# A hybrid encoder block on one core: front, attention and experts' start reordered, operands placed alike

## The reference

```python
mod = silu(c) @ w_ada + b_ada            # 6 vectors of 1024 per group
h = rmsnorm(x) * (1 + scale1) + shift1
proj = h @ w_in                          # 5648 columns
#   qkv_a, z_a, beta, alpha: DeltaNet, 4 heads of 128, both directions, chunks of 64
#   q_b, k_b, v_b: 8 heads of 64, attention in a window of 8 rows x 16 columns of the 8 x 64 grid
merged = sigmoid(gate_a) * (o_a @ w_oa) + sigmoid(gate_b) * (o_b @ w_ob)
x = x + gate1 * (merged @ w_out)
h = rmsnorm(x) * (1 + scale2) + shift2
#   16 experts, each takes its top 64 tokens of each group:
y[idx] += (silu(h[idx] @ w_gate) * (h[idx] @ w_up)) @ w_down * gate
x = x + gate2 * y;  out = rmsnorm(x)
```

## Time and profile before

| | us |
|---|---|
| median of three runs | 2578.36 |
| lowest, highest | 2576.54, 2578.36 |
| the profiled execution's own time | 2572.44 |
| its span | 2570.7 |

### The profile page before, as it was taken

How to read it: one execution, slowest core, us unless ns; L and a number is a source line. 1 busy time by engine, 2 the same in 40 slices (tenths; PEclk the granted TensorE clock), 3 DMA queues, 4 the chain that set the end, 5 groups by cost and what they waited for, 6 DMA issues and landing times. The chain is left out here.

```text
span 2570.7 us, 39210 instructions
## 1 busy us (share of the span) xinstructions
PE 2389.5 (93%) x15048; PEld 1815.6 (71%) x15048; DVE 1508.4 (59%) x1785; ACT 1166.5 (45%) x1296; POOL 447.8 (17%) x396
## 2 busy tenths in 40 slices
PE   4999998899998999989992999999999999999994
PEld 2777887777776777743452888888888888888883
DVE  4566212555553333312115788888888888888884
ACT  4232222222222333321112667776776776767772
POOL 5110202232321000011232011111101111111101
PEclk8999999999998999999995999999999999999997
DMA  7446621001002122164314899999999999999994
GB/s 272 148 141 179 159 79 43 19 20 34 19 31 74 63 86 67 37 234 163 115 66 175 320 369 380 373 372 373 371 370 375 381 376 380 373 376 373 373 363 147
DMA packets 266048, 556.95 MB, mean 217 GB/s; under 512 B 13256, under 2 KB 66605, under 8 KB 262861
## 3 DMA queue, kind: packets, MB, share of 16 engines
q1 hardware_dynamic: 256717, 530.15, 57.4%
q0 software_dynamic: 4608, 16.78, 2.6%
q10 hardware_dynamic: 4608, 8.39, 0.9%
HBM read 511.21 MB, written 44.07 MB: 216 GB/s over the span
## 5 line engine op out<-in xcount | busy, mean ns | idle before, releaser
L2378 PE MATMUL ps<-whigh,xeT 128*128 128x512 f32 x2048 | 668.9, 400 | 9.0 <-DVE xeT L2523 9.0
L2531 DVE TENSOR_TENSOR wlow<-hT,whigh 128x2048 fp32r<-128x2048 f32 x192 | 431.9, 2284 | 84.5 <-ACT whigh L2474 84.5
L2378 PEld LDWEIGHTS ps<-whigh,xeT 128*128 128x128 f32 x2048 | 387.0, 189 | 100.1 <-issue 9.4
L2378 PE MATMUL ps<-wlow,xeT 128*128 128x512 f32 x1024 | 406.6, 397 | 0.0
L2474 ACT ACTIVATE whigh<-hT 128x2048 fp32r<-128x2048 f32 x192 | 358.6, 1911 | 17.8 <-PE ps L2378 17.8
L2378 PE MATMUL ps<-whigh,hidT 128*128 128x512 f32 x1024 | 334.6, 398 | 1.5 <-DVE hidT L2558 1.5
L2531 DVE TENSOR_TENSOR wlow<-oaT,whigh 128x2048 fp32r<-128x2048 f32 x96 | 216.7, 2285 | 50.2 <-ACT whigh L2474 50.2
L2531 DVE TENSOR_TENSOR wlow<-obT,whigh 128x2048 fp32r<-128x2048 f32 x96 | 217.8, 2284 | 29.6 <-ACT whigh L2474 29.6
L2378 PEld LDWEIGHTS ps<-whigh,hidT 128*128 128x128 f32 x1024 | 192.8, 188 | 47.9 <-issue 1.7
L2378 PEld LDWEIGHTS ps<-wlow,xeT 128*128 128x128 f32 x1024 | 193.6, 189 | 43.2
L2378 PE MATMUL ps<-wlow,hidT 128*128 128x512 f32 x512 | 202.8, 396 | 0.0
(11 more groups left out here) (289 smaller groups left out, 3542.4 us busy)
## 6 DMA issues: line engine op xcount, KB each, us to landing
hT<-in_w_down SPq DMA_DIRECT2D x66, 1024.0 KB, 8.8
obT<-in_w_up SPq DMA_DIRECT2D x64, 1024.0 KB, 8.7
hT<-in_w_up SPq DMA_DIRECT2D x64, 1024.0 KB, 6.4
hT<-in_w_gate SPq DMA_DIRECT2D x62, 1024.0 KB, 9.3
oaT<-in_w_down SPq DMA_DIRECT2D x62, 1024.0 KB, 7.2
oaT<-in_w_gate SPq DMA_DIRECT2D x34, 1024.0 KB, 9.3
obT<-in_w_gate SPq DMA_DIRECT2D x32, 1024.0 KB, 5.9
oaT<-in_w_ada SPq DMA_DIRECT2D x20, 1024.0 KB, 7.8
```

Of the source, the lines that this page charges most:

```text
L2378: mm = pe.matmul(out, lhs[x], rhs[y], start=start and i == 0, stop=stop and i == 2)
L2531: dve.tensor_tensor(wlow[slot][:, :], raw[(FIRST + x) % RAW_SLOTS], whigh[slot][:, :].bitcast(F32), ALU.subtract).then_inc(low_done, 1)
```

## The change

- **Front stage.** A sixth buffer for pieces of w_ada, over the third and fourth weight tile's raw buffers. SP loads five pieces, tile 0, three pieces, tile 1, and tile 2 once piece 5 is multiplied. The out_t buffers move ahead of w_high, so that w_high0 and w_low0 lie over pieces 2 and 3. split(0) waits for four pieces only and stands before the copy of modrow on ScalarE and before the mod vectors on VectorE. The mod_dram stores are issued at tile 20.
- **Its end.** The front awaits only the stores of DeltaNet's tiles. DeltaNet's first vnew, which with wT lies over out_t, waits for the others, and SP does before it loads attention's first pair.
- **Attention.** A unit's head is now its fastest index, so units 2s and 2s + 1 are the two heads of one pair on the same tile. A slot s has scores of both, eight gate products, both turns, eight, both values, eight. Sums and reciprocals have four places, the values of a pair one bank.
- **Experts.** ScalarE makes whigh of three pieces and VectorE wlow of two before their parts of xeT, and the other three and four after them.
- **Addresses.** Two unused buffers of 32 bytes, and the places of wg and gst, move ghi and glo to 32 modulo 64, as h_high is, and xeT and hidT to 0 modulo 64, as whigh is.

```diff
-    ADA_SLOT = [0, 1, 2, 3, 4, 0, 1, 4] + [q % 2 for q in range(8, PIECES)]
+    ADA_SLOT = [0, 1, 2, 3, 4, 5, 0, 1] + [q % 2 for q in range(8, PIECES)]
...
+        ada.append(m["obT"][:, 2:4, :].rearrange("p h t -> p (h t)"))
...
-                for q in range(KD):
+                for q in range(5):
                     load_ada(q)
-                for tile in range(3):
-                    load_tile(sp, a, wraw, w_in, tile)
+                load_tile(sp, a, wraw, w_in, 0)
+                for q in range(5, KD):
+                    load_ada(q)
+                load_tile(sp, a, wraw, w_in, 1)
+                sp.wait_ge(ada_ps, 6)
+                load_tile(sp, a, wraw, w_in, 2)
...
+                    if tile == 20:
+                        for part in range(2):
+                            sp.wait_ge(mod_done, part + 1)
+                            for b in range(4):
+                                c = (ADA_FIRST + 4 * part + b) * ADA_BLOCK
+                                sp.dma_start(mod_dram[:, c:c + ADA_BLOCK], brow[32 * b:32 * b + GROUPS, part, :]).then_inc(mod_out, 16)
...
-                    sp.wait_ge(out_kept[i], 16 * NU // 4)
+                    sp.wait_ge(out_kept[i], 16 * GROUPS * A_TILES // 4)
...
+                act.wait_ge(ada_ps, 4)
+                split(0)
                 act.wait_ge(ada_ps, KD)
                 act.activation(modrow[:, :], ps[:, 7, :], ACT.Copy).then_inc(modrow_sb, 1)
                 act.wait_ge(mul_ready, 5)
                 act.wait_ge(xT_dve, KD // 2)
                 act.wait_ge(xT_act, KD // 2)
-                for k in range(4):
-                    high(0, k)
-                split(0)
-                for k in range(4, KD):
+                for k in range(KD):
...
-                        dve.wait_ge(ada_ps, KD)
+                        dve.wait_ge(ada_ps, 4)
...
+                split(0)
...
+                        elif d == 0:
+                            for i in range(4):
+                                act.wait_ge(first["out_kept"][i], 16 * GROUPS * PROJ_TILES // 4)
...
+        sb("same_offset_g", [P, 8])
...
+            t, hp = divmod(r, 2)
...
+                for s in range(SLOTS):
+                    if s < NPAIR:
+                        scores(2 * s)
+                        scores(2 * s + 1)
+                    if s in V_AT:
+                        turn_v(*V_AT[s])
+                    if s < NPAIR:
+                        gates(TERMS // 3)
+                    if 1 <= s < NPAIR + 1:
+                        turn(2 * s - 2)
+                        turn(2 * s - 1)
+                    if s < NPAIR:
+                        gates(TERMS // 3)
+                    if 2 <= s < NPAIR + 2:
+                        values(2 * s - 4)
+                        values(2 * s - 3)
+                    if s in OUT_AT:
+                        turn_out(*OUT_AT[s])
+                    if s < NPAIR:
+                        gates(TERMS // 3)
                 assert not list(products)
...
+                for s in range(SLOTS):
+                    if 1 <= s < NPAIR + 1:
+                        keep_gate(s - 1)
+                    if s in V_AT:
+                        h, g = V_AT[s]
                         act.wait_ge(vt_ps, GROUPS * h + g + 1)
                         if h >= 1:
                             act.wait_ge(pv_ps, PER_PAIR * (h - 1) + (g + 1) * 2 * TPG)
                         act.activation(vtok[:, g, :, :], ps[:, 0, :], ACT.Copy).then_inc(vtok_sb, 1)
-                    if w < NW:
-                        h, g, hp, t = unit(w)
-                        act.wait_ge(low_done, w + 1)
-                        if w >= 2:
-                            act.wait_ge(pT_ps, w - 1)
-                            act.wait_ge(rden_done, w - 1)
-                        act.activation(pr[:, w % 2, 0:width(t)], sc[:, w % 2, 0:width(t)], ACT.Exp, scale=-1.0,
-                                       bias=low[:, w % 2:w % 2 + 1],
-                                       accum_out=den[:, w % 2:w % 2 + 1]).then_inc(exp_done, 1)
-                        if w % 2 == 1:
-                            keep_gate(w // 2)
-                        if w % 4 == 1 and w // 4 + 1 < GTILES:
-                            split(w // 4 + 1)
-                    if 1 <= w < NW + 1:
-                        v = w - 1
-                        h, g, hp, t = unit(v)
-                        act.wait_ge(pT_ps, v + 1)
-                        if v >= 2:
-                            act.wait_ge(pv_ps, v - 1)
-                        act.activation(pT[:, v % 2, 0:width(t)], ps[:, 4 + v % 2, 0:width(t)], ACT.Copy).then_inc(pT_sb, 1)
+                    if 1 <= s < NPAIR + 1:
+                        keep_probs(2 * s - 2)
+                        keep_probs(2 * s - 1)
+                    if s < NPAIR:
+                        expose(2 * s)
+                        expose(2 * s + 1)
+                        if s % 2 == 0 and s // 2 + 1 < GTILES:
+                            split(s // 2 + 1)
...
+        sb("same_offset_e", [P, 8])
...
-                for x in range(-FIRST, AHEAD):
+                for x in range(-FIRST, 1):
                     high(0, x)
                 tokens(0, 7, 1)
                 tokens(1, 4, 2)
+                for x in range(1, AHEAD):
+                    high(0, x)
...
-                for x in range(-FIRST, AHEAD):
+                for x in range(-FIRST, 0):
                     low(0, x)
                 tokens(0, 7, 1)
                 tokens(1, 4, 2)
+                for x in range(0, AHEAD):
+                    low(0, x)
```

More of the change, by code:

```diff
@@ L164, in first_buffers @@
     first["w_in"] = [sem(f"w_in{i}") for i in range(4)]
+    first["out_kept"] = [sem(f"out_kept{i}") for i in range(4)]
     first["rel_in"] = sem("rel_in")
@@ L229, in phase_front @@
         xt = m["xt"]
+        out = [sb(f"out_t{i}", [P, SEQ]) for i in range(4)]
         whi = [sb(f"w_high{i}", [P, KD, P], F32R) for i in range(3)]
@@ L283, in phase_front @@
         xT_dve = sem("xT_dve")
-        ada_in = [sem(f"ada_in{i}") for i in range(5)]
+        ada_in = [sem(f"ada_in{i}") for i in range(6)]
         ada_ps = sem("ada_ps")
@@ L299, in phase_front @@
         silu_done = sem("silu_done")
-        out_kept = [sem(f"out_kept{i}") for i in range(4)]
+        out_kept = first["out_kept"]
         pads = sem("pads")
@@ L930, in sem @@
             return sems[-1]
+        vnew = [sb(f"vnew{d}", [P, TPG, P]) for d in range(2)]
+        wT = [sb(f"wT{d}", [P, TPG, 2, CHUNK]) for d in range(2)]
         qn = sb("qn", [P, TPG, P])
@@ L946, in phase_deltanet @@
         inv = [sb(f"inv{d}", [P, 2, TPG, CHUNK]) for d in range(2)]
-        wT = [sb(f"wT{d}", [P, TPG, 2, CHUNK]) for d in range(2)]
-        vnew = [sb(f"vnew{d}", [P, TPG, P]) for d in range(2)]
         state = [spare[:, 4 * SEQ + d * TOK:4 * SEQ + (d + 1) * TOK].rearrange("p (i c) -> p i c", i=NCHUNK) for d in range(2)]
-        junk = m["gate2"][:, 0:P]
+        junk = sb("junk_d", [P, P])
         ssqo = sb("ssqo", [P, TPG])
@@ L1029, in _ @@
                     load_z(sp, conv_dram, first, n)
+                for i in range(4):
+                    sp.wait_ge(first["out_kept"][i], 16 * GROUPS * PROJ_TILES // 4)
                 sp.wait_ge(tokv_ps, NU)
@@ L1737, in values @@
                     pe.wait_ge(pT_sb, w + 1)
-                    if w >= 2:
-                        pe.wait_ge(otok_done, w - 1)
+                    if w >= 4:
+                        pe.wait_ge(otok_done, w // 2 * 2 - 2)
                     for i in range(k1 - k0):
-                        mm = pe.matmul(ps[:, 6 + w % 2, 0:DH], pT[:, w % 2, i * P:(i + 1) * P],
+                        mm = pe.matmul(ps[:, 6 + w // 2 % 2, w % 2 * DH:(w % 2 + 1) * DH], pT[:, w % 2, i * P:(i + 1) * P],
                                        vtok[:, g, k0 + i, hp * DH:(hp + 1) * DH], start=(i == 0), stop=(i == k1 - k0 - 1))
                     mm.then_inc(pv_ps, 1)
-                for w in range(SLOTS):
-                    if w < NW:
[L1747 to L1757, removed]
+                for s in range(SLOTS):
[18 more added lines that the diff above has]
+                        gates(TERMS // 3)
                 assert not list(products)
@@ new lines, in biased @@
+                def biased(w):
+                    h, g, hp, t = unit(w)
+                    n = width(t)
+                    if g == 0 and t == 0:
+                        dve.wait_ge(bias_done, 6 * h + 3 * (hp + 1))
+                    dve.wait_ge(s_ps, w + 1)
+                    if w >= 2:
+                        dve.wait_ge(exp_done, w - 1)
+                    at = KIND_AT[KIND_OF[t]]
+                    dve.tensor_tensor(sc[:, w % 2, 0:n], ps[:, 2 + w % 2, 0:n], bias[:, hp, at:at + n],
+                                      ALU.subtract).then_inc(sc_done, 1)
+                    dve.wait_ge(sc_done, w + 1)
```

(21 more changed lines are left out.)

96 lines of the change are left out of this document (39 added, 57 removed).

## The result

The changed kernel takes 2545.7 us in the median (2536.46 to 2552.05, four runs) where the kernel before takes 2578.36: a ratio of 0.9869, 95% interval 0.9851 to 0.9887. It is faster by 1.3%, where 2.8% were forecast; 2545.7 lies outside the range of 2498 to 2535. The profiled execution has 2544.42 us of its own and a span of 2542.7, 28.0 less than before, for a forecast of 71.

A forecast was written before the change was run, and what follows sets the result against it. TensorE, busy for 93% of the span, was taken to bound the kernel. Terms 5.2 + 3.2 + 22.1 + 7.5 + 33 = 71 us off the profiled 2572.4 gave 2501.4, plus 5.9 for the median: 2507, range 2498 to 2535.

The forecast's parts named there:

- front, start: Front: a sixth w_ada buffer ends the mod pieces 4.4 us earlier, plus 0.8 from the first split; 5.2 us.
- front, end: Front to DeltaNet: waits for the last stores move later, so DeltaNet starts at 409.0 for 412.2; 3.2 us.
- attention: Attention: paired scores, quicker gate products and joint turns, less added boundaries and a bank wait; 22 us, bounds 7.8 and 24.
- experts, start: Experts: fewer splits ahead of xeT bring the first product from 1410.16 to 1402.7; 7.5 us, bounds 5 and 8.
- experts, pace: Experts: equal starts modulo 64 bytes quicken 4608 steps by 0.0074 us each; 33 us taken, bounds 0 and 34.
- Rival one: Attention and experts: addresses are not the cause of the pace, so 33 + 5.2 us go; 2546 us, chance 0.12.
- overlap in row halves: Attention: two heads' scores run at once in upper and lower 64 rows, 0.67 or 0.89 us a pair; 21.8 us.
- rival four: Attention: pairs meet a new wait, as the gates' copy, 0.7 us in 32 pairs; 22 us, 2530, chance 0.04.
- the 5.2 us of pace: Attention: equal starts modulo 64 bytes quicken 768 gate products by 0.0068 us each; 5.2 us saved.
- the boundaries: Attention: three runs of eight gate products for two of twelve, 0.18 us a boundary in 32 pairs; 5.8 us lost.
- Rival three: Experts: the queues bind, an expert takes 68.6 us, so 11 us go; 2518 us, chance 0.14.

The follow-up runs named there:

- no_pads: The changed kernel without the two unused 32-byte buffers; 2549.67 us.
- best256: copy_first with ghi, glo, xeT and hidT moved so that all operands of the products by parts start equal modulo 256 bytes; 2506.12 us.
- one_run: best256 with a slot's 24 gate products in one run behind scores, turns and values, instead of three runs of eight; 2499.86 us.
- before_experts256: The kernel before plus 416 unused bytes ahead of the experts' tokens, so the experts' operands start alike modulo 256; 2544.65 us.
- survey1: The changed kernel with padding for several weight-to-column distances (front 0, 128, 256; attention 0, 64; experts 0, 256 bytes); 2514.46 us, one run.
- copy_first: The changed kernel, but VectorE copies attention's turned output (obT) before making glo of the next gate tile; 2532.67 us.
- waits_back: copy_first with the front's end awaiting all stores and the experts' first six splits ahead of the tokens' parts again; 2545.22 us, one run.

## Why the prediction was wrong

| step | forecast, us | measured, us |
|---|---|---|
| front, start | 5.2 | 4.2 |
| front, end | 3.2 | 3.3 |
| DeltaNet | 0 | -4.3 |
| attention | 22 | 13.75 |
| merge and route, finish | 0 | -0.2 |
| experts, start | 7.5 | 7.6 |
| experts, pace | 33 | 3.6 |
| sum | 71 | 28.0 |

- **The step that failed** is "what differs is the addresses: in the front weights and columns both start at 32 modulo 64 bytes". The cause was rightly seen in the addresses, but three stretches fitted many rules, and I took the one that the change aims at. Equal modulo 256 is what the front had and what the change doesn't make: it moves the distance from 96 to 128. The runs showed 0.2341 at 96, 0.2332 at 128 and 0.227 at 0 and 256, so the buffers gave 0.9 ns a step instead of 7.4: about 4 us (3.6 between the two kernels' stages, 4.05 against no_pads) of 33. The pace itself, once had, took 29.85 us off the 4608 steps; 34.1 were worked out, as if no step were slow after a break.
- **Rival one** named 2546, the measured time, for a cause that the runs refute: addresses are the cause. That its number came true is chance; it needs every other term as forecast, and attention and DeltaNet were not. The Trainium skill's page SBUF — State Buffer, section A bandwidth-pool intuition that's wrong (but worth ruling out), gives the weight loads a read port of their own, which no run here shows or denies. That start addresses then cost nothing was the prediction's conclusion, not the page's, and the one padded line that took 29.85 us off the experts refutes it.
- **Attention.** The overlap in row halves was right: 0.70 and 0.92 for a pair, where 0.67 and 0.89 were forecast. The Trainium skill's page TensorE: Matmul & The Clock Gate says in Part 3: Packing small matmuls — row/col tiling that products in different row groups run at once. The trace agrees: 0.92 us for a pair in two halves, 1.34 for one in the same rows. Two things were missed. One is the new wait of 11.1 us. I had looked for one in the gates' copy (rival four), where the view of waits shows only 2.7 us; it lay in a bank that the turns of values and of outputs share, behind an instruction order on an engine called idle. The other is that the 5.2 us of pace can't be had in runs of eight. The eighth product of a run starts 1.721 us after the first in the kernel before, 1.712 in the changed one and 1.698 in best256; an estimate from these is 96 runs x 0.009 = 0.9 us for the change and 2.2 for equal starts. Without the wait attention gained 24.9 us, more than forecast less the pace, so another term was too dear. The likeliest are the boundaries, put at +5.8: one_run has two fewer in each of 32 slots and took 7.8 us less, 0.12 each where 0.18 was forecast, pace included. No run splits the rest.
- **Rival three** is refuted: in before_experts256, with steps at 0.227, TensorE still idles for only 1.5 us in the experts, and 380 GB/s are moved between 1700 and 1770. Its price had a slip as well: 68.6 us is a third of the way from 67.9 to the rate of 70.0, not half; halfway would be 17 us, inside the range all the same.
- **Front, start.** The mod sum came at 41.67, and the ninth piece of w_ada is 5.9 us earlier (64.3 for 70.2). From some 112 us on only 4.2 are left: in the changed kernel the granted clock is 0.50 between 112 and 115, which is 1.2 GHz, where in the kernel before it stays at 1.00 from 100 to 127. TensorE was busy throughout, before the fall as well; what made it fall stays open.

```profile
112.00:115.00 3.00, 3.00 (x8) 2.34 (x7) 0.00 (x0) 0.00 (x0) 0.00 (x0) 0.50 1.02 383
```

- **DeltaNet.** The stage takes 380.47 us before and 384.74 after. The changed kernel's DeltaNet took 376.85 in survey1, 377.49 in no_pads, 384.78 in copy_first and 386.52 in waits_back, at granted clocks from 0.95 down to 0.92, so the same code varies by more than the 4.3 us. But seven of its ten traces lie between 384 and 387, and the two of the kernel before's at 380; a small cost of the change itself is not excluded. What decides whether the clock dips there stays open. The changed kernel's four runs spread over 15.6 us, the quickest at a mean granted clock of 0.969 and the slowest at 0.960; in which stage they differ is not known.

## What to carry to other kernels

When the same instruction runs at two paces, compare every address modulo larger powers of two and vary the distance on purpose: several distances fit in one program, and one padded buffer tried on the kernel before would have told the term of 33 us. When an engine with idle time gets work in a new order, follow each of its instructions on which a shared PSUM bank hangs; a wait placed ahead of it costs what the busy engine then idles. Put products that profit from a steady pace into long runs.

## What the hardware showed that was not expected

- The distance between the starts of a product's weights and columns sets the pace of 128x128 by 512 products in the rounded format. It is 0.227 us at 0 and 256 bytes and 0.233 at 32, 64, 128, 160 and 224 in the front. The 0.227 comes with the DMA engines' share at 0.35 in the front and at 1.03 in the experts alike. In the experts 224 gave 0.233 too, 192 lay between (0.229), and 96 gave 0.2341.
- After a break the first step takes about 0.315 us, and the next eight take 0.230 on average even with equal starts; only then comes a steady 0.227 (best256, one_run).
- The granted clock of DeltaNet, a stage with gaps, was 0.92 to 0.95 in traces of the same code, and the stage took 376.85 to 386.52 us.
